# Gated mixing reordered on VectorE, page numbers read ahead, and waits behind norms split in two

## What is computed

```python
h = x + 0.5 * g1 * swiglu(modulate(x, g_ffn1, s1, sc1), w1_gate, w1_up, w1_down)
n = modulate(h, g_mix, s2, sc2)                      # rmsnorm, then times (1 + scale), plus shift
u, q, k, v, qi, ki, wi, g_c, g_a = split_in(n, w_in, ...)
conv_out = conv_branch(u_ext, w_dw, b_dw, ln_g, ln_b, w_conv_out)
att = attend(q, k, v, qi, ki, wi).reshape(B, T, ATT_DIM) @ w_attn_o
mix = (sigmoid(g_c) * conv_out + sigmoid(g_a) * att) @ w_out
h = h + g2 * mix
h = h + 0.5 * g3 * swiglu(modulate(h, g_ffn2, s3, sc3), w2_gate, w2_up, w2_down)
```

## Time and profile before

| | |
|---|---|
| median of three, us | 2641.59 |
| profiled execution, us | 2641.7 |
| its span, us | 2639.9 |
| TensorE busy | 2485.7 us, 94% |
| GpSimd busy | 1458.6 us, 55% |
| VectorE busy | 1401.2 us, 53% |
| ScalarE busy | 662.7 us, 25% |
| granted TensorE clock, mean | 0.97 |

### The profile page before, as it was taken

The page is one execution under the profiler, slowest core; times in us unless marked ns, Lnnn a source line. Parts: engine busy times, 40 slices in busy tenths (PEclk is TensorE's granted clock), DMA queues, the critical chain, the costliest instruction groups (busy, mean ns, idle before and its releaser), DMA issues.

```text
span 2639.9 us, 44639 instructions
## 1 busy us (share of the span) xinstructions
PE 2485.7 (94%) x16038; PEld 2307.2 (87%) x16038; DVE 1401.2 (53%) x2619; ACT 662.7 (25%) x1238; POOL 1458.6 (55%) x1234
## 2 busy tenths in 40 slices
PE   5999999999998888899999779999899999999997
PEld 3899999999997756699998446789799999999997
DVE  5543334434446638799998445462564444444444
ACT  3311011111112323335544457310511111111113
POOL 1276666666665325536999020124057777777774
PEclk8999999999999879999999969999999999999999
DMA  8422222222221532231224600334011111111112
GB/s 288 120 68 77 72 67 68 79 79 79 73 79 53 151 74 77 75 102 49 79 92 145 220 11 1 98 98 146 1 33 48 49 53 50 53 49 48 48 48 82
DMA packets 243128, 209.99 MB, mean 80 GB/s; under 512 B 14687, under 2 KB 207315, under 8 KB 241993
## 3 DMA queue, kind: packets, MB, share of 16 engines
q1 hardware_dynamic: 232844, 181.70, 22.9%
q10 hardware_dynamic: 10181, 26.90, 3.2%
HBM read 173.03 MB, written 28.94 MB: 77 GB/s over the span
## 4 chain that ended last, share of the span: by engine, by line
PE 82%; DVE 6%; issue 4%; SPq 3%; ACT 3%; POOL 1%; DMA 0%; ACTq 0%; DVEq 0%; POOLq 0%
PE main L763 11%; PE main L764 10%; PE main L765 10%; PE main L295 7%; PE main L296 7%; PE main L297 7%; PE main L864 5%; PE main L865 5%; PE main L866 5%; SPq L1925 2%; DVE pick L1742 2%; PE main L2144 2%; PE main L2161 1%; PE aux L2172 1%; PE aux L763 1%
## 5 line engine op out<-in xcount | busy, mean ns | idle before, releaser
L684 POOL TENSOR_TENSOR blo<-raw,bhi 128x512 fp32r<-128x512 f32 x424 | 553.5, 1306 | 34.0
L682 POOL CAST bhi<-raw 128x512 fp32r<-128x512 f32 x424 | 264.7, 624 | 544.8 <-PE main L866 311.4
L763 PE MATMUL main<-nhi,bhi 128*128 128x352 f32 x1312 | 429.1, 327 | 17.9 <-issue 10.8
L764 PE MATMUL main<-nlo,bhi 128*128 128x352 f32 x1312 | 423.0, 322 | 0.0
L765 PE MATMUL main<-nhi,blo 128*128 128x352 f32 x1312 | 422.8, 322 | 0.0
L295 PE MATMUL main<-nhi,whi 128*128 128x352 f32 x1032 | 340.3, 330 | 1.0 <-DVE pick_s L1730 0.5
L297 PE MATMUL main<-nhi,wlo 128*128 128x352 f32 x1032 | 334.1, 324 | 0.0
L296 PE MATMUL main<-nlo,whi 128*128 128x352 f32 x1032 | 334.1, 324 | 0.0
L1100 DVE SCALAR_TENSOR_TENSOR h<-main,ada,h 128x352 f32<-128x352 f32 (+1 forms) x448 | 251.9, 570 | 84.5 <-PE main L866 84.5
L864 PE MATMUL main<-hid_hi,bhi 128*128 128x352 f32 x896 | 292.1, 326 | 4.7 <-DVE h L1100 2.8
L282 POOL CAST whi<-raw 128x1024 fp32r<-128x1024 f32 x51 | 56.4, 1106 | 422.0 <-issue 234.6
(11 more groups left out here) (379 smaller groups left out, 5130.7 us busy)
## 6 DMA issues: line engine op xcount, KB each, us to landing
raw<-in_w_gate SPq DMA_DIRECT2D x44, 512.0 KB, 4.1
raw<-in_w_up SPq DMA_DIRECT2D x44, 512.0 KB, 3.9
ada_part<-in_w_ada SPq DMA_DIRECT2D x44, 512.0 KB, 5.0
raw<-in_w_down SPq DMA_DIRECT2D x44, 512.0 KB, 3.9
raw<-in_w_in SPq DMA_DIRECT2D x40, 512.0 KB, 3.9
ada_raw<-in_w_ada SPq DMA_DIRECT2D x7, 2048.0 KB, 12.0
gate_d<-zraw ACTq DMA_DIRECT2D x16, 528.0 KB, 2.7
gates<-gate_d SPq DMA_DIRECT2D x16, 528.0 KB, 4.7
```

Source lines behind the costliest of these rows:

```text
L682: pool.tensor_copy(bhi[:, slot], src).then_inc(sg.block_hi.sem, 1)
L684: pool.tensor_tensor(blo[:, slot], src, bhi[:, slot].bitcast(F32), ALU.subtract)\
L763: pe.matmul(out, bhi[:, slot, w], hi(c), start=start and c == 0, stop=False, skip_group_check=True)
L764: pe.matmul(out, bhi[:, slot, w], lo(c), start=False, stop=False, skip_group_check=True)
```

## The change

Three edits. In the mixing, VectorE's loop is written out, and the low part of chunk n - 1 is made after the two gated products of chunk n and ahead of their sum. Sixteen page numbers are read once into registers, one behind each of the last sixteen weight loads of the projection, and used for key and value pages. `ready` takes a half, and TensorE waits for the first half's low part before work on it and for the second before work on that; in the mixer's first projection the second wait stands in the middle of a product.

```diff
-            def ready(pe, t):
-                norm_wait(pe, q, "lo", 2 * t + 2)
+            def ready(pe, t, half=1):
+                norm_wait(pe, q, "lo", 2 * t + half + 1)
...
                     for m in range(2):
-                        if m == 0:
-                            nrm["ready"](pe, t)
                         for half in range(2):
+                            if m == 0:
+                                nrm["ready"](pe, t, half)
                             sg.block_ready.wait(pe, 2 * m + half + 1)
...
             for L in range(Z_Q + 1, NZ):
                 load_tile(sp, T_Z + L, L % RING, cols(w_in, ZCOL[L]))
+                n = L - (NZ - 2 * NSEQ)
+                if n >= 0:
+                    page_of.append(sp.value_load(a["page_table"][n // 2:n // 2 + 1, n % 2:n % 2 + 1], min_val=0,
+                                                 max_val=L0["cache_k"].shape[0] - 1))
...
-                    norm_m["ready"](pe, t)
-                    z_product(pe, L, T_Z + L, L % RING, 3 * L, L % 2, 72 if L == 0 else P, ts=(t,))
+                    norm_m["ready"](pe, t, L)
+                    z_product(pe, L, T_Z + L, L % RING, 3 * L, L % 2, 72 if L == 0 else P, ts=(t,),
+                              middle=(lambda t: norm_m["ready"](pe, t)) if L == 0 else None)
...
-                    page = sp.value_load(a["page_table"][b:b + 1, pg:pg + 1], min_val=0,
-                                         max_val=cache.shape[0] - 1)
-                    sp.dma_start(dst[:, pg, :], cache[bass.ds(page, 1)].rearrange("o p h d -> (o p) (h d)"))\
+                    sp.dma_start(dst[:, pg, :], cache[bass.ds(page_of[2 * b + pg], 1)].rearrange("o p h d -> (o p) (h d)"))\
...
-            with dve.Fori(0, KD // 2) as i:
...
+            def mix_low(n):
+                m, t = n // NTC, n % NTC
+                dve.wait_ge(mix_hi, n + 1)
+                dve.tensor_tensor(nlo[:, m, tcs(t)], mixt[:, n % 2, 0, :], nhi[:, m, tcs(t)].bitcast(F32),
+                                  ALU.subtract).then_inc(mix_lo, 1)
+
+            for n in range(NTC * KD):
+                m, t = n // NTC, n % NTC
+                x, y = mixt[:, n % 2, 0, :], mixt[:, n % 2, 1, :]
+                if t == 0:
+                    dve.wait_ge(g_in[m % 2], 32 * (m // 2) + 32)
+                dve.wait_ge(acc_done, ACC_MIX + 6 * m + 3 + t + 1)
+                if n >= 2:
+                    dve.wait_ge(mix_lo, 2 + n - 1)
+                dve.tensor_tensor(x, main[:, (ACC_MIX + 2 * t) % NBANK, 0:TC], gates[:, m % 2, 0, tcs(t)], ALU.mult)\
+                    .then_inc(mix_a, 1)
+                dve.tensor_tensor(y, main[:, (ACC_MIX + 2 * t + 1) % NBANK, 0:TC], gates[:, m % 2, 1, tcs(t)],
+                                  ALU.mult).then_inc(mix_free, 1)
+                if n:
+                    mix_low(n - 1)
+                dve.wait_ge(mix_free, 3 + n + 1)
+                dve.wait_ge(mix_a, 3 * n + 1)
+                dve.tensor_tensor(x, x, y, ALU.add).then_inc(mix_a, 2)
+            mix_low(NTC * KD - 1)
```

More of the change, by code:

```diff
@@ L1239, in piece_at @@
             return range(n, n + 2) if L > Z_Q and n < len(PIECES) else range(0)
+        page_of = []
         def m1_sp(sp):
```

## The result

The changed kernel takes 2611.48 us in the median of four runs (2609.21 to 2618.93) against 2643.03 for the kernel before on the same chip: a ratio of 0.9886 (95% interval 0.9866 to 0.9906). Forecast were 2612 us, range 2603 to 2620. The profiled execution of after took 2609.24 us, its span is 2607.4 instead of 2639.9. In this and the later tables the ratio is an estimate from all runs of both kernels and can differ from the quotient of the two medians by up to 0.002; one run of the kernel before in the last group of experiments took 7702 us, nearly three times as long as any other, and is left out of every figure here.

What follows compares the result with a forecast made beforehand. TensorE carries 82% of the chain of work, and the edits touch places where it waits. Off 2641.7 us go 11.6 + 13.0 + 3.3 + 1.65 + 0 = 29.6 us, giving 2612 us, range 2603 to 2620.

Steps and rivals of the forecast that it cites:

- Mixing: Mixing of the branches: new order ends TensorE's waits for VectorE's gated products; 11.6 us off, 6 to 12.
- the sentence on the straight code: Mixing: VectorE's loop is now straight code; its fetch, not shown for this stage, has the 2.7 us of cover too.
- The hold: Mixing: GpSimd's weight split might hold VectorE's products, costing 5.6 us of the gain; none assumed, 5.6 kept for the range.
- Pages: Cached pages: page numbers in registers end TensorE's wait for value pages; attention starts 13.0 us earlier, low bound 10.
- Rivals 3 and 4: Transfers, not reads, pace the pages: 2624 us, chance 0.05; reads in the projection delay weight loads: 2660 us, chance 0.02.
- First norm: Start of the product behind the first norm: TensorE waits only for the first half; 3.3 us off, 0 to 4.
- Mixer norm: Product behind the mixer norm: TensorE starts after the first of the last chunk's two low parts; 1.65 us off.
- with the clock coming back a step sooner: Mixer norm: upper bound of its range, 3.3 us off, if TensorE's clock also recovers a step earlier.
- Last norm: Product behind the last norm: TensorE's earlier start becomes a longer wait for ScalarE; 0 off, 1.0 lost to 1.9 gained.
- Rival 1: Start of attention: without the gap TensorE's clock stays at 2.4 GHz, at most 9 us more, 2603 us; chance 0.11.
- rival 2: Gains swallowed: norm starts taken back by ScalarE or VectorE, or queued outputs hold the pages; 2615 to 2620 us, chance 0.17.

Runs made afterwards that it cites:

- mix_old_order: Kernel before with the mixing loop as straight code and the change's waits, each low part directly behind its own add; 2631.94 us, ratio 0.9953.
- halves_only: Kernel before with only the waits by halves of the change; 2638.24 us, ratio 0.9976.
- warm: Changed kernel with 15 matmuls of constants into a free bank in TensorE's idle times around the start of attention; 2615.78 us, ratio 0.988.
- values_read: Changed kernel with the old page-number read ahead of each of the sixteen value pages, none ahead of key pages; 2615.67 us, ratio 0.9897.
- new_order_later: Kernel before with only the mixing edit, plus one VectorE product of 0.43 us ahead of the middle chunk's products; 2638.75 us, ratio 0.9972.

## Why the prediction was right, step by step

- **Mixing, 11.6 us: right in size, half right in cause.** X to N lost 11.67 us: 7 x 1.56 = 10.9 in the tiles and 0.75 at the end, where I took 0.6. The third chunk's products end 0.9 us behind the tile's end (I said 1.1). The step that failed is the sentence on the straight code: I weighed its fetch as a cost and never asked what it saves. It saves 0.24 us a chunk, and that alone removes the wait (`mix_old_order`, splits 11.45 us apart). A reader should have been warned by the earlier trace rows: the add misses the split's start by 0.28 us.
- **The hold.** I took none for the products and kept 5.6 us for the range. Products beside the cast took 0.51 us (1681.40), and in the last norm L1029, with one of its two inputs in PSUM like the products, took 0.52 in the middle of the subtraction from 1882.10, while adds and low parts took up to 2.71. The Trainium skill, "SBUF — State Buffer", section "Who interferes with whom", states that a VectorE instruction with two inputs in SBUF contends with a GpSimd instruction that reads SBUF, and that one with at most one such input, outside the two-port modes (`tensor_tensor` has none), does not. The trace agrees with both (0.51 and 0.52 us, and 2.71), and by it the 5.6 us need not have been kept for the mixing's low bound.
- **Pages, 13.0 us: right.** 13.9 from C to A, of which 13.2 lie between the two selections, where 13.08 of idle time was to go. The issue of one page was put at 0.65 us; it takes 4.40 / 8 = 0.55 for the first eight key pages and 14.16 / 16 = 0.89 for the values, without effect, with 19 us to spare. Rivals 3 and 4 did not occur.
- **First norm, 3.3 us: right** (3.26). The second half's low part ended before it was wanted.
- **Mixer norm, 1.65 us: the step itself right (1.60), the term mis-sized.** F to C gained 5.1 us (4.3 in medians). I allowed 3.3 in all "with the clock coming back a step sooner". Up to the first product behind this wait 1.27 went, from there to C 3.86 (549.68 us instead of 553.54). In its first 6 us the granted clock is 0.72 instead of 0.56, and over the 233.6 us up to 1116 and 1120 us it is 0.92 instead of 0.90; behind that it is 1.00 in both. My estimate from these two means is 233.6 x 0.02 = 4.7 us, with their rounding 2 to 7, so the clock can account for the 3.86 us, and with it for the 3.5 beyond my term (2.7 in medians). It comes with the waits by halves (`halves_only` has 1371.03 from F to C), but no run isolates the clock.
- **Last norm, 0: mis-sized.** The low bound (1.0 lost) named the right mechanism, GpSimd's splits freed earlier, though what they meet is the combinations behind the low part; its price is 1.3 us. The wait for ScalarE that I said would grow did, from 1.08 to 3.50 us.
- **Sum.** 32.5 us of span went where 29.6 were forecast: 3.5 more from F to C, 0.9 more in the pages, 0.3 in mixing and attention; 1.2 less in the last norm, and 0.5 less at the start, where VectorE's first low part came 0.46 us later. The median fell by 31.6, but from 2643.03, where I had counted from 2641.59. That 2611.48 lies half a microsecond from 2612 is in part luck: the misses go both ways, and the runs of one kernel differ by 10 us.
- **Rivals 1 and 2.** Rival 1 did not occur: the clock stayed at 1.2 GHz (granted 0.50) from 1513 to about 1541 us, and that the idle time costs the clock, as I argued, `warm` shows by filling it (1.00). Of rival 2 only the last norm's 1.3 us came.

## What to carry to other kernels

Where an engine waits in every turn of a loop for another that meets a third at a fixed moment, read how far each operation misses that moment: a tenth of a microsecond can decide between 13.0 and 11.45 us a turn, and a gain that rests on it vanishes with 0.43 us of additional work, while one that puts the operations that can be held behind those that free the buffer doesn't (11.45 us apart with and without that work). Register reads from memory ahead of a DMA (1.7 us here against 0.4 for the DMA's issue) belong in an idle stretch of the same queue, and those of the transfers that stand ahead in the queue count too, here for more than the values' own (8.7 and 4.5 us). A wait that is split so that one engine starts earlier also starts its followers earlier: look at what they then meet.

## What the runs showed of the hardware

- The same instructions get different granted clocks in the same place: from C to the first selection the kernels with unchanged order took 70.6 to 74.8 us. One trace doesn't compare this stage to within 3 us.
- Fifteen matmuls whose results nobody reads, put into idle times, raised the granted clock at its start from 0.50 to 1.00 and made the attention stage 7 to 8 us shorter (136.56 us against 143.5 and 144.52); seven of them made it 5.9 us shorter. Neither shows in the time of the whole kernel.
- In VectorE's mixing loop a chunk takes 0.24 us more than in straight code with the same order (2.93 and 2.69): 0.10 between the second product and the add, 0.15 between the add and the low part.
- The hold goes both ways: GpSimd's cast takes 1.04 us in the loop, but 1.29 in `mix_old_order`, where VectorE's add, with both inputs in SBUF, started 0.13 us ahead of it, and 1.16 in `new_order_later`, where one started 0.26 us ahead.
- With a register read ahead of each (`values_read`), sixteen value pages leave within 41 us, with the numbers in registers within 14.
